# Turning softmax probabilities in a float32 mixer: a product with a scaled diagonal, or an in-place scaling and a plain transpose

## The chip, the cores and the metric

The kernel runs on one core of a Trainium2 chip. The metric is the device time of one execution in microseconds. "Line" numbers are those of the kernel before.

## What is computed

The reference sends 256 tokens of width 1024 (float32, batch 1) through a first block (retention, a linear recurrent unit, a gated feed-forward part) and then through two layers of a second block: feed-forward, hybrid mixer, feed-forward. The mixer has three branches on one input projection: gated linear attention (GLA), a causal depthwise convolution of 31 taps followed by a layer norm and silu, and sliding-window attention (8 query heads of width 64 on 2 key heads, window 128, blocks of 128, ALiBi, and one sink logit per head). For the window attention the reference computes, per head,

```python
s = jnp.einsum('bnqhgd,bnkhd->bnhgqk', qb, kk).astype(jnp.float32) * (DH ** -0.5)
s = s - slopes[:, :, None, None] * dist.astype(jnp.float32)
s = jnp.where(valid[None, :, None, None], s, -jnp.inf)
p = jax.nn.softmax(jnp.concatenate([s, sink], axis=-1), axis=-1)[..., :-1]
o = jnp.einsum('bnhgqk,bnkhd->bnqhgd', p.astype(v.dtype), vv)
```

The first query block has only its own 128 keys; the second has 256.

## The kernel before, in words

All weights are streamed from HBM in units of 1 MB (`raw`, three slots). ScalarE copies each unit to `w_hi` with a rounded type (`hi`, line 581), VectorE forms the rest `w_lo = raw - w_hi` (`lo`, line 963), and TensorE multiplies each tile three times (hi*hi, lo*hi, hi*lo). SP's queue loads unit c as soon as VectorE has split unit c - 3 (`fill`, line 388). The same two-part split is made of every activation operand (`operand_hi`, `operand_lo`: `b_hi`, `b_lo`).

Each engine has its program written out by hand, in order, with semaphores between them; nothing is reordered at run time. The mixer of layer l stands from line 1440 (VectorE), line 856 (ScalarE), line 541 (GpSimd) and from line 1958 on (TensorE); units cm to cm + 8 are its input projection, cm + 9 to cm + 12 its output projection. "Bank n" is the PSUM bank `stream[(gm + n) % 3]` in which TensorE leaves the n-th group of outputs.

The window attention is worked in two halves b = 0, 1 of four score rows each. `ss` holds, for every one of 8 slots, three blocks of 128 scores, each followed by a sink column (129 columns a block): two blocks for the second query block and one for the first. A half goes through these steps:

- VectorE adds the ALiBi table to the scores (`window_scores`, line 1472), takes the row maxima (`softmax_shift`, line 1493), and ScalarE applies the exponential in place and sums each row (`exponentials`, line 860; `ss_exp`).
- VectorE (`softmax_scale`, line 1507) takes the reciprocals of the eight row sums, waits for GpSimd's `ke_ready`, and writes eight scaled identity matrices (128x128 each) into `ek[:, 0, b]`; then it signals `p_ready`.
- TensorE (`probabilities`, line 1985) makes twelve float32 products, each with a 128x128 block of `ss` as the stationary operand and a scaled identity as the moving one. That transposes a block and divides it by its row sums at once. It signals `pt_full`; ScalarE copies the twelve tiles to `pt` (`turned_probabilities`, line 868).
- When both halves are there and all taps are done, TensorE multiplies them by the values (`window_out`, line 2098), and ScalarE and VectorE split the result for the output projection.

Among these steps, VectorE works on the taps of the convolution's first 128 channels (`conv(first, to)`, line 1444, one instruction a tap), the evacuation of bank 8 into `gr` (the GLA gate, `read_pair(8, ...)`), the head variance for GpSimd (`var8`, line 1567), the gate (line 1572), the head norm (lines 1577 and 1582) and the split of weight units (`lo`). TensorE takes the taps of the other 128 channels as products with diagonal matrices (`conv_taps`, line 1972, one tap is one float32 product of 256 columns). The order on TensorE around the change (lines 2080 to 2126) is: taps, head statistics, first half's probabilities, six taps, second half's probabilities (behind a wait for bank 8's evacuation), the roots of the heads (behind GpSimd's `rstd8_ready`), the remaining taps, `window_out` (behind both halves' copies). The output projection follows (`deep_pass`, line 1702), and between its passes the convolution's mean, variance and root.

The order on VectorE (lines 1559 to 1575):

```python
window_scores(1)
softmax_shift(1)
softmax_scale(0)
lo(cm + 10)
conv(9, 17)
dve.wait_ge(group_evac, gm + 8)
read_pair(8, gr[:, :, :], 1.0)
dve.wait_ge(stat_full, st0 + ST_GLA + 1)
V.tensor_scalar(var8[:, :], psm[:, 3, 0:8], RMS_EPS, None, ALU.add).then_inc(var8_ready, 1)
softmax_scale(1)
conv(17, 22)
```

Elsewhere the kernel turns tiles with `nc.tensor.transpose`: the residual (`turn`, line 1726, lines 1728 to 1733) and the hidden activations (line 1895), always one 128x128 tile a call.

Of the kernel before, what the change touches and what calls it, by code (L numbers as in the profile page):

```python
# [21 lines left out]
ALU = mybir.AluOpType  # L22
AX = mybir.AxisListType.X

P = 128
T = 256
TT = T // P
# [168 lines left out]
def build(nc, io, out):  # L196
    with ExitStack() as ctx:  # L197
# [23 lines left out]
        ident, means, headsel = const("ident"), const("means"), const("headsel")  # L221
# [45 lines left out]
        ek = sb("ek", [P, 2, TT, LEV, P], scope=m2)  # L267
# [6 lines left out]
        ss = sb("ss", [P, SWH, 3 * (P + 1)], scope=m2)  # L274
        mx = sb("mx", [P, 4, 16], scope=m2)
# [6 lines left out]
        def keys(slot, n):  # L282

            return ss[:, slot, n * (P + 1):n * (P + 1) + P]

        def mx_half(row, b):

            return mx[:, row, 8 * b:8 * b + 8]
# [43 lines left out]
        ez_ready, lev_ready, e_ready, qe_ready, ke_ready, zeroed, gate_ready = (sem(n) for n in (  # L332
            "ez_ready", "lev_ready", "e_ready", "qe_ready", "ke_ready", "zeroed", "gate_ready"))
# [5 lines left out]
        up_ready, diag_loaded, dve_tap, pe_taps, gla_full, gla_free, ss_ready, ss_exp, p_ready = (sem(n) for n in (  # L339
            "up_ready", "diag_loaded", "dve_tap", "pe_taps", "gla_full", "gla_free", "ss_ready", "ss_exp", "p_ready"))  # L340
# [607 lines left out]
        def _(dve):  # L948
            V = nc.vector
# [128 lines left out]
            ins = V.tensor_copy(vecs[:, :, :], stream[2][:, :].rearrange("p (g c) -> p g c", g=4))  # L1078
# [47 lines left out]
            for n in range(4):  # L1126
# [9 lines left out]
                if n == 2:  # L1136
                    dve.wait_ge(psm_full, PSM_SC + 1)
                    for h in range(HEADS):
                        ins = V.tensor_tensor(st_ret[:, 384 * h:384 * h + 384], psm[:, h, 0:384], ret_d[:, h, :], ALU.mult)
                    ins.then_inc(psm_free, 1)  # L1140

            at = [0] * KT
            for n in range(4):
# [4 lines left out]
                if n == 0:  # L1148
                    dve.wait_ge(psm_full, PSM_O + 1)
                    for h in range(HEADS):  # L1150
                        ins = V.tensor_copy(o_ret[:, 2 * h:2 * h + 2, :], pair2(psm[:, h, :]))
                    ins.then_inc(psm_free, 1)
                if n < 3:
                    tap = 2 - n
                    for k in range(KT):
                        if n == 0:
                            dve.wait_ge(lru_conv0, k + 1)
                        else:
                            dve.wait_ge(dve_chain, at[k])
                        col = V1["lconv_w"] + 8 * tap + k  # L1160
                        ins = V.scalar_tensor_tensor(out=xc[:, k, :], in0=xl[:, k, tap:tap + T],
                                                     scalar=vecs[:, 0, col:col + 1], in1=xc[:, k, :],
                                                     op0=ALU.mult, op1=ALU.add)
# [14 lines left out]
            for b in range(2):  # L1178
                ins = V.tensor_tensor(heads(o_ret, b), heads(o_ret, b), over_halves(b), ALU.subtract)
            ins.then_inc(psm_free, 1)  # L1180
            for n in range(4):
# [8 lines left out]
                if n == 2:  # L1190
                    dve.wait_ge(psm_full, PSM_VAR + 1)
                    for b in range(2):
                        ins = V.tensor_tensor(heads(o_ret, b), heads(o_ret, b), over_halves(b), ALU.mult)
                    ins.then_inc(psm_free, 1)
            for n in range(8):
# [3 lines left out]
                for f in range(2):  # L1199
                    k = 2 * (n % 4) + f  # L1200
                    if n < 4:
                        ins = V.tensor_scalar(la[:, k, :], la[:, k, :], 1.0, sp4[:, k:k + 1], ALU.add, ALU.mult)
                    else:
                        ins = V.scalar_tensor_tensor(out=i_gate[:, k, :], in0=i_gate[:, k, :], scalar=1.0,
                                                     in1=xc[:, k, :], op0=ALU.add, op1=ALU.mult)
# [6 lines left out]
            for k in range(KT):  # L1212
                ins = V.scalar_tensor_tensor(out=o_ret[:, k, :], in0=o_ret[:, k, :], scalar=half_b[:, 32 + k:33 + k],
                                             in1=g_ret[:, k, :], op0=ALU.mult, op1=ALU.mult)
# [212 lines left out]
            for l in range(LAYERS):  # L1427
# [9 lines left out]
                at = ffn(c0, 2 * l, N_L + 3 * l)  # L1437
# [6 lines left out]
                def conv(first, to):  # L1444

                    dve.wait_ge(up_ready, l + 1)
                    for tap in range(first, to):
                        acc = (yc[:, 0, :], yc_sum[:, :])[tap % 2]
                        x, w = up[:, 0, tap:tap + T], vec("conv_w", 2 * tap)
                        if tap > 1:  # L1450
                            dve.wait_ge(dve_tap, TAPS * l + tap - 1)
                        if tap == 0:
                            ins = V.tensor_scalar(acc, x, w, vec("conv_b", 0), ALU.mult, ALU.add)
                        elif tap == 1:
                            ins = V.tensor_scalar(acc, x, w, None, ALU.mult)
                        else:
                            ins = V.scalar_tensor_tensor(out=acc, in0=x, scalar=w, in1=acc, op0=ALU.mult, op1=ALU.add)
                        ins.then_inc(dve_tap, 1)
# [28 lines left out]
                def read_pair(n, dst, scale):  # L1487

                    dve.wait_ge(unit_used, USED[cm + n])
                    V.scalar_tensor_tensor(out=dst, in0=pair2(bank(n)[:, :]), scalar=scale, in1=over2(rb[:, :]),  # L1490
                                           op0=ALU.mult, op1=ALU.mult).then_inc(group_evac, 1)
# [15 lines left out]
                def softmax_scale(b):  # L1507

                    dve.wait_ge(ss_exp, 2 * l + b + 1)
                    link(V.reciprocal(mx_half(3, b), mx_half(0, b)))  # L1510
                    dve.wait_ge(ke_ready, TT * (l + 1))
                    V.tensor_tensor(ek[:, 0, b, :, :], ident.rearrange("p (o i) -> p o i", o=1).broadcast_to([P, 8, P]),
                                    mx_half(3, b).rearrange("p (n o) -> p n o", o=1).broadcast_to([P, 8, P]),
                                    ALU.mult).then_inc(p_ready, 1)

                inv_rms(ps70 + PS7_RB)
                dve.wait_ge(pool_init, 4)
# [42 lines left out]
                softmax_shift(1)  # L1560
                softmax_scale(0)
                lo(cm + 10)
                conv(9, 17)
                dve.wait_ge(group_evac, gm + 8)
                read_pair(8, gr[:, :, :], 1.0)
                dve.wait_ge(stat_full, st0 + ST_GLA + 1)
                V.tensor_scalar(var8[:, :], psm[:, 3, 0:8], RMS_EPS, None, ALU.add).then_inc(var8_ready, 1)
                softmax_scale(1)
                conv(17, 22)
                dve.wait_ge(group_evac, gm + 9)  # L1570
                dve.wait_ge(gr_th, l + 1)
                V.scalar_tensor_tensor(out=gr[:, :, :], in0=th2[:, :, :], scalar=1.0, in1=gr[:, :, :],
# [3 lines left out]
                for f in range(2):  # L1576
                    ins = V.scalar_tensor_tensor(out=og[:, f, :], in0=og[:, f, :], scalar=vec("gla_g", f),
                                                 in1=psm[:, 3, f * T:f * T + T], op0=ALU.mult, op1=ALU.mult)
# [22 lines left out]
                for f in range(2):  # L1601
                    ins = V.scalar_tensor_tensor(out=yc[:, f, :], in0=yc[:, f, :], scalar=vec("ln_g", f),
                                                 in1=cbank[:, T:2 * T], op0=ALU.mult, op1=ALU.mult)
# [33 lines left out]
        def _(pe):  # L1637
            passed = {"n": 0}

            def mm(dst, lhs, rhs, start, stop):  # L1640
                return nc.tensor.matmul(dst, lhs, rhs, start=start, stop=stop, skip_group_check=True)  # L1641
# [278 lines left out]
            for l in range(LAYERS):  # L1920
# [12 lines left out]
                def cols(tile, n):  # L1933
                    return tile[:, n * P:n * P + P]
# [50 lines left out]
                def probabilities(b, banks):  # L1985

                    pe.wait_ge(p_ready, 2 * l + b + 1)
                    for n in range(12):
                        slot, key, at = (n // 2, n % 2, n // 2) if n < 8 else (n - 8, 2, n - 4)
                        ins = mm(cols(banks[n // 4], n % 4), keys(4 * b + slot, key), ek[:, 0, b, at, :],  # L1990
                                 n % 4 == 0, n % 4 == 3)
                    ins.then_inc(pt_full, 1)

                def value(h):
# [209 lines left out]
```

## Time and profile before

| | |
|---|---|
| time, median of 3 runs | 1498.53 us (1496.96 to 1499.06) |
| the profiled execution's own time | 1498.52 us |
| span of that execution, first to last instruction | 1496.4 us |
| mean granted clock of TensorE | 0.997 of full speed |
| TensorE (PE) busy | 1467.3 us, 98% |
| VectorE (DVE) busy | 969.7 us, 65% |
| ScalarE (ACT) busy | 711.6 us, 48% |
| GpSimd (POOL) busy | 35.7 us, 2% |
| HBM | 172 GB/s over the span |

All times inside the trace count from the start of the span. PE is the row of matrix products and transposes, PEld that of the loads of their stationary operand. A start time and a duration are given for each instruction; instructions overlap in their pipelines, so what an instruction costs its engine in a dense row is the distance from its start to the next start, and not its duration. A group "x24" has the start of its first instruction and the time to the end of its last. The bracket at the end of a row is the idle time of the engine ahead of it and what ended it.

### The profile page before, as it was taken

The page shows a single profiled execution, that of the slowest core. Times are in us where ns is not written, and L with a number is a line of the kernel's source. Part 1 is how long each engine was busy: PE and PEld are TensorE (multiplying, and loading weights), DVE is VectorE, ACT ScalarE, POOL GpSimd, SP SyncE. Part 2 cuts the span into 40 slices and gives each one's busy share as a digit, 9 for nine tenths or more (in the row PEclk, how much of TensorE's full clock was granted, in tenths as well). Part 3 has the DMA queues.
Part 4 walks back from the last instruction along what each step waited for, and adds up shares of the span by engine and source line. Part 5 has one row for each costly group of instructions (what it writes and reads, how often), then busy time and mean ns, then how long its engine had stood idle before and what let it go on. Part 6 is the DMA issues. An engine that isn't in the chain of part 4 may idle for free. (4 is left out here: it accounts for less than half of the span.)

```text
span 1496.4 us, 21713 instructions
## 1 busy us (share of the span) xinstructions
PE 1467.3 (98%) x9104; PEld 1287.5 (86%) x9104; DVE 969.7 (65%) x1195; ACT 711.6 (48%) x878; POOL 35.7 (2%) x50
## 2 busy tenths in 40 slices
PE   7999999999999999999999999999999999999998
PEld 7999999899988788888987888878888889788886
DVE  5867786688864766546876665556664578666644
ACT  5433863555543544436345444354444534454442
POOL 0000000000000000001000000000000010000000
PEclk9999999999999999999999999999999999999999
DMA  7735465666655576456414755547755452365542
GB/s 249 234 120 163 147 197 192 174 179 187 180 197 169 183 225 212 154 194 148 155 57 141 219 189 183 183 143 250 225 183 185 132 136 99 113 208 179 190 156 97
DMA packets 253460, 259.15 MB, mean 173 GB/s; under 512 B 26659, under 2 KB 217524, under 8 KB 253364
## 3 DMA queue, kind: packets, MB, share of 16 engines
q1 hardware_dynamic: 252480, 255.49, 53.8%
q10 hardware_dynamic: 884, 2.28, 0.4%
q8 instruction: 72, 1.18, 0.3%
q14 instruction: 24, 0.20, 0.0%
HBM read 256.69 MB, written 1.05 MB: 172 GB/s over the span
## 5 line engine op out<-in xcount | busy, mean ns | idle before, releaser
L970 DVE TENSOR_TENSOR w_lo<-raw,w_hi 128x2048 fp32r<-128x2048 f32 x240 | 545.0, 2273 | 339.1 <-ACT w_hi L588 338.8
L588 ACT ACTIVATE w_hi<-raw 128x2048 fp32r<-128x2048 f32 x240 | 456.4, 1902 | 342.9 <-PE psm L1641 139.3
L1641 PE MATMUL stream<-a_hi,w_hi 128*128 128x256 f32 x1072 | 307.6, 287 | 2.9 <-DVE a_lo L989 1.8
L1641 PE MATMUL stream<-a_lo,w_hi 128*128 128x256 f32 x1072 | 304.6, 284 | 0.0
L1641 PE MATMUL stream<-a_hi,w_lo 128*128 128x256 f32 x1072 | 304.5, 284 | 0.0
L1641 PE MATMUL stream<-w_hi,a_hi 128*128 128x512 f32 (+1 forms) x640 | 243.6, 381 | 8.0 <-DVE w_lo L970 5.7
L1641 PE MATMUL stream<-w_hi,a_lo 128*128 128x512 f32 (+1 forms) x640 | 239.3, 374 | 0.0
L1641 PE MATMUL stream<-w_lo,a_hi 128*128 128x512 f32 (+1 forms) x640 | 238.8, 373 | 0.0
L1641 PEld LDWEIGHTS stream<-a_hi,w_hi 128*128 128x128 f32 x1072 | 206.7, 193 | 4.8 <-issue 3.2
L1641 PEld LDWEIGHTS stream<-a_lo,w_hi 128*128 128x128 f32 x1072 | 207.2, 193 | 0.0
L1641 PEld LDWEIGHTS stream<-a_hi,w_lo 128*128 128x128 f32 x1072 | 207.0, 193 | 0.0
L1641 PE MATMUL psm<-w_hi,h_hi 128*128 128x512 f32 x448 | 178.3, 398 | 0.0
L1641 PE MATMUL psm<-w_hi,h_lo 128*128 128x512 f32 x448 | 177.5, 396 | 0.0
L1641 PE MATMUL psm<-w_lo,h_hi 128*128 128x512 f32 x448 | 177.5, 396 | 0.0
L1641 PEld LDWEIGHTS stream<-w_hi,a_hi 128*128 128x128 f32 x640 | 120.5, 188 | 30.9 <-DVE w_lo L970 8.3
L1641 PEld LDWEIGHTS stream<-w_hi,a_lo 128*128 128x128 f32 x640 | 120.5, 188 | 22.0
L1641 PEld LDWEIGHTS stream<-w_lo,a_hi 128*128 128x128 f32 x640 | 120.7, 189 | 19.9
L1641 PEld LDWEIGHTS psm<-w_hi,h_lo 128*128 128x128 f32 x448 | 84.4, 188 | 20.6
L1641 PEld LDWEIGHTS psm<-w_lo,h_hi 128*128 128x128 f32 x448 | 84.4, 188 | 20.1
L1641 PEld LDWEIGHTS psm<-w_hi,h_hi 128*128 128x128 f32 x448 | 84.4, 188 | 20.1
L811 ACT ACTIVATE gu<-stream,rs 128x256 f32<-128x256 f32 x68 | 32.1, 472 | 72.2 <-PE stream L1641 72.2
L1641 PE MATMUL ps<-w_hi,a_hi 128*128 128x512 f32 x160 | 62.6, 391 | 0.0
(282 smaller groups left out, 1575.9 us busy)
## 6 DMA issues: line engine op xcount, KB each, us to landing
raw<-in_ffn_w_up SPq DMA_DIRECT2D x136, 512.0 KB, 5.0
raw<-in_ffn_w_down SPq DMA_DIRECT2D x104, 512.0 KB, 4.5
raw<-in_ffn_w_gate SPq DMA_DIRECT2D x88, 512.0 KB, 4.0
raw<-in_w_in SPq DMA_DIRECT2D x80, 512.0 KB, 4.6
raw<-in_w_out SPq DMA_DIRECT2D x24, 512.0 KB, 4.4
raw<-in_w_ret_o SPq DMA_DIRECT2D x8, 512.0 KB, 4.2
raw<-in_w_lru_o SPq DMA_DIRECT2D x8, 512.0 KB, 4.0
diag<-in_conv_diag SPq DMA_DIRECT2D x8, 512.0 KB, 5.8
```

The source lines that it names most:

```text
L588: nc.scalar.activation(w_hi[s][:, :, 0:n], raw[s][:, :, 0:n], ACT.Copy).then_inc(w_hi_ready, 1)
L811: nc.scalar.activation(th_t[:, 2 * (g % 2) + t, :], up_bank(g, t)[:, 0:UC], ACT.Tanh, scale=rs4[:, 2 + t:3 + t]).then_inc(th_ready, 1)
L970: V.tensor_tensor(w_lo[s][:, :, 0:n], raw[s][:, :, 0:n], w_hi[s][:, :, 0:n].bitcast(F32), ALU.subtract).then_inc(w_split, 1)
L1641: return nc.tensor.matmul(dst, lhs, rhs, start=start, stop=stop, skip_group_check=True)
```

## The change

The eight scaled identities are no longer made. VectorE multiplies the probabilities themselves by the reciprocals, in place in `ss`: one instruction for the four rows of 257 columns (two blocks and the sink column between them), one for the four rows of 128. The wait for `ke_ready` in this step is dropped. TensorE turns each block with `nc.tensor.transpose` and the plain identity. On VectorE the second half's scaling is moved ahead of the evacuation of bank 8, and the taps 9 to 16, which stood together ahead of the evacuation, stand behind it: 9 to 11 ahead of the head variance, 12 to 21 behind it.

```diff
--- before.py
+++ after.py
@@ -1508,10 +1508,11 @@
 
                     dve.wait_ge(ss_exp, 2 * l + b + 1)
                     link(V.reciprocal(mx_half(3, b), mx_half(0, b)))
-                    dve.wait_ge(ke_ready, TT * (l + 1))
-                    V.tensor_tensor(ek[:, 0, b, :, :], ident.rearrange("p (o i) -> p o i", o=1).broadcast_to([P, 8, P]),
-                                    mx_half(3, b).rearrange("p (n o) -> p n o", o=1).broadcast_to([P, 8, P]),
-                                    ALU.mult).then_inc(p_ready, 1)
+                    for row, first, n in ((0, 0, 2 * P + 1), (4, 2 * P + 2, P)):
+                        probs = ss[:, 4 * b:4 * b + 4, first:first + n]
+                        over = mx[:, 3, 8 * b + row:8 * b + row + 4].rearrange("p (n o) -> p n o", o=1)
+                        ins = V.tensor_tensor(probs, probs, over.broadcast_to([P, 4, n]), ALU.mult)
+                    ins.then_inc(p_ready, 1)
 
                 inv_rms(ps70 + PS7_RB)
                 dve.wait_ge(pool_init, 4)
@@ -1560,13 +1561,13 @@
                 softmax_shift(1)
                 softmax_scale(0)
                 lo(cm + 10)
-                conv(9, 17)
+                softmax_scale(1)
                 dve.wait_ge(group_evac, gm + 8)
                 read_pair(8, gr[:, :, :], 1.0)
+                conv(9, 12)
                 dve.wait_ge(stat_full, st0 + ST_GLA + 1)
                 V.tensor_scalar(var8[:, :], psm[:, 3, 0:8], RMS_EPS, None, ALU.add).then_inc(var8_ready, 1)
-                softmax_scale(1)
-                conv(17, 22)
+                conv(12, 22)
                 dve.wait_ge(group_evac, gm + 9)
                 dve.wait_ge(gr_th, l + 1)
                 V.scalar_tensor_tensor(out=gr[:, :, :], in0=th2[:, :, :], scalar=1.0, in1=gr[:, :, :],
@@ -1986,9 +1987,8 @@
 
                     pe.wait_ge(p_ready, 2 * l + b + 1)
                     for n in range(12):
-                        slot, key, at = (n // 2, n % 2, n // 2) if n < 8 else (n - 8, 2, n - 4)
-                        ins = mm(cols(banks[n // 4], n % 4), keys(4 * b + slot, key), ek[:, 0, b, at, :],
-                                 n % 4 == 0, n % 4 == 3)
+                        slot, key = (n // 2, n % 2) if n < 8 else (n - 8, 2)
+                        ins = nc.tensor.transpose(cols(banks[n // 4], n % 4), keys(4 * b + slot, key), ident)
                     ins.then_inc(pt_full, 1)
 
                 def value(h):
```

## Rows read from the trace of the kernel before

**Rows 1.** The page, part 1: busy us, share of the span, instructions.

```profile
PE 1467.3 (98%) x9104; PEld 1287.5 (86%) x9104; DVE 969.7 (65%) x1195; ACT 711.6 (48%) x878; POOL 35.7 (2%) x50
```

**Rows 2.** Busy time, 750 to 787: window; PE, PEld, DVE, ACT, POOL; PEclk, DMA, GB/s.

```profile
750.00:787.00 37.00, 37.00 (x275) 32.22 (x275) 27.00 (x49) 15.71 (x34) 2.34 (x2) 1.00 0.18 58
```

**Rows 3.** Timeline of PE in both mixers: start, duration, line, operation, out<-in, count.

```profile
757.62 2.92 PE L1641 MATMUL psm<-ek,ss 128*128 128x128 f32 x24
760.39 2.76 PE L1641 MATMUL ps<-up,diag 128*128 128x256 f32 x12
762.98 2.84 PE L1641 MATMUL stream<-ek,ss 128*128 128x128 f32 x24
765.75 1.09 PE L1641 MATMUL psm<-keep,rstd 128*64 128x128 f32 x16
...
771.29 3.11 PE L1641 MATMUL stream<-pt,vs 128*64 128x128 f32 x48
...
1258.80 2.92 PE L1641 MATMUL psm<-ek,ss 128*128 128x128 f32 x24
```

**Rows 4.** Timeline of PE: the turn of the residual's first half, projection.

```profile
796.34 0.60 PE L1732 MATMUL stream<-keep,x_t 128*128 128x128 f32 x4
796.77 0.60 PE L1732 MATMUL ps<-keep,x_t 128*128 128x128 f32 x4
797.12 0.48 PE L1641 MATMUL psm<-w_hi,b_hi 128*128 128x512 f32 x1
```

**Rows 5.** Tile x_t, PEld, 780 to 1000: duration ns min/median/max.

```profile
L1732 PEld LDWEIGHTS psm<-keep,x_t x16: 138/140/143, 806.0 to 997.3; 128*128 128x128 f32 x16
```

**Rows 6.** Timeline of DVE in the first mixer.

```profile
751.16 1.22 DVE L1512 TENSOR_TENSOR ek<-keep,mx 128x1024 f32<-128x1024 f32 x1
752.30 2.28 DVE L970 TENSOR_TENSOR w_lo<-raw,w_hi 128x2048 fp32r<-128x2048 f32 x1
754.50 0.48 DVE L1457 SCALAR_TENSOR_TENSOR yc_sum<-up,vecs,yc_sum 128x256 f32<-128x256 f32 x1
...
757.67 0.68 DVE L1490 SCALAR_TENSOR_TENSOR gr<-stream,rb 128x512 f32<-128x512 f32 x1
758.27 0.15 DVE L1567 TENSOR_SCALAR var<-psm 128x8 f32<-128x8 f32 x1
...
762.79 0.69 DVE L1572 SCALAR_TENSOR_TENSOR gr<-th,gr 128x512 f32<-128x512 f32 x1 [1.01 <-ACT th L912]
...
766.89 0.87 DVE L1577 SCALAR_TENSOR_TENSOR og<-og,vecs,psm 128x256 f32<-128x256 f32 x2 [1.44 <-PE psm L1641]
...
771.47 0.68 DVE L977 TENSOR_TENSOR b_lo<-hn,b_hi 128x512 fp32r<-128x512 f32 x1
...
772.98 0.43 DVE L1591 TENSOR_TENSOR yc<-yc,yc_sum 128x256 f32<-128x256 f32 x1
775.07 1.29 DVE L977 TENSOR_TENSOR b_lo<-stream,b_hi 128x512 fp32r<-128x512 f32 x2 [1.66 <-ACT b_hi L636]
```

**Rows 7.** Timelines of ACT and of POOL in the first mixer.

```profile
754.49 0.19 ACT L864 ACTIVATION_READ_ACCUMULATOR ss<-ss,mx 128x1 f32 x1
...
760.59 1.57 ACT L872 ACTIVATE pt<-psm 128x512 f32<-128x512 f32 x3 [4.95 <-PE psm L1641]
...
758.51 1.64 POOL L530 TENSOR_TENSOR rstd<-var,mhalf 128x8 f32<-128x8 f32 x1 [44.35 <-DVE var L1567]
```

**Rows 8.** Timeline of PE: channel mean of the convolution, first product of unit 12.

```profile
775.13 1.02 PE L1641 MATMUL stream<-yc,keep 128*128 128x256 f32 x4
...
788.05 0.47 PE L1641 MATMUL psm<-w_hi,b_hi 128*128 128x512 f32 x1 [0.28 <-DVE b_lo L977]
```

**Rows 9.** Timeline of DVE: the split of unit 13.

```profile
795.82 2.29 DVE L970 TENSOR_TENSOR w_lo<-raw,w_hi 128x2048 fp32r<-128x2048 f32 x1 [1.77 <-ACT w_hi L588]
```

**Rows 10.** Busy time of PE: window; PE; PEclk, DMA, GB/s.

```profile
15.00:20.00 5.00, 3.98 (x17) 0.67 0.99 357
796.00:798.00 2.00, 2.00 (x15) 1.00 0.00 0
```

## The prediction

> **What bounds the kernel now.** I read the page's first part first: TensorE is busy for 98% of the span and VectorE for 65% [rows 1]. Busy time alone proves nothing, since the ends of matmuls are modelled, so the next view is the busy time in the stretch of the first mixer that the change touches: over 37 us from 750 TensorE shows no idle time, at a granted clock of 1.00, while VectorE idles 10 us of it [rows 2]. The timelines of the single engines say why. TensorE goes straight from one group into the next: twelve products "psm<-ek,ss" in 24 records, six taps, twelve more products, the head roots, ten taps, the output products, the projection [rows 3]. None carries an idle bracket; in this stretch the time is the sum of what TensorE has to issue. The second layer shows the same groups, the first of them 501.18 us later and just as long [rows 3], so each term below counts twice.
>
> Two facts in these rows make the estimate. A float32 product of 128 columns takes **two records** (24 for 12), and 24 records occupy 2.77 us: 757.62 to 760.39 in the first half, 762.98 to 765.75 in the second [rows 3], or 0.231 us a product. A float32 transpose of the same size takes **one record**: a turn of the residual, two groups of four, runs from 796.34 to 797.12 [rows 4]. That is 0.78 us for eight; I add 0.10 us as my own allowance for the switch back to products, which gives 0.88 us, 0.110 each. Both forms have the data as the stationary operand and something in `keep` or `ek` as the moving one, so the change alters the mode, not the roles.
>
> **The change, part by part.**
>
> *Products become transposes (TensorE, on the path).* Removed per half: 2.77 us. Added: 12 x 0.110 = 1.32 us. Saved: 1.45 us a half, 2.90 a layer, 5.80 in all. Bounds: at worst a transpose is held to the 140 ns of its weight load [rows 5], 12 x 0.140 = 1.68, saving 1.09 a half (4.4 in all); at best the second group's pace, (797.12 - 796.77) / 4 = 0.0875, saving 1.72 a half (6.9). I take 0.110, since it covers eight transposes with the switch after them, nearest to twelve in a row.
>
> The row gives one record instead of two, a factor of 2.1. The Trainium skill (TensorE: Matmul & The Clock Gate, Terms) says that transpose mode is "4× faster for FP32". By that figure the two halves of both layers would save 4 x (2.77 - 0.69) = 8.3 us; the rows here speak for half that speed, and the sum goes by them.
>
> *Scaling the probabilities in place instead of a diagonal (VectorE, hidden, but barely).* Removed per half: one multiply of 1024 elements, 1.22 us, which holds the engine 1.14 us until the next starts (751.16 to 752.30) [rows 6]. Added: one of 1028 and one of 512. The nearest rows for 512 are the 128x512 subtraction at 771.47, 0.68 us long, and the 128x512 multiply at 757.67, which lets the next start after 0.60 [rows 6]. So a half holds VectorE 0.60 us longer, 1.20 a layer; without overlap it would be 0.68, and 0.08 more if the strided rows of the in-place form cost a start-up each. Less than 0.60 has no row in its favour, since cost goes by elements. What hides it: VectorE idles 1.01 us ahead of the gate (for ScalarE's tanh) and 1.44 us at the head norm (for TensorE's roots) [rows 6].
>
> *What the idle time becomes.* Before, VectorE reached the gate at 762.79 - 1.01 = 761.78; now at 762.98. ScalarE's tanh stands behind its copy of the turned first half, which starts at 760.59 as the products end [rows 7]; with them 1.45 us earlier, tanh ends near 761.2, so the gate waits for nothing and starts 0.19 late. The head norm was reached at 766.89 - 1.44 = 765.45; now at 765.64, and TensorE's roots, 2.90 us earlier, are done by then. It starts 1.24 us earlier than before, and all that follows on VectorE in order with it: two taps, the split of unit 11, the split of the first operand, two taps, the sum `yc`. That sum ended at 772.98 + 0.43 = 773.41 and would end at 772.17 [rows 6].
> TensorE's use of it, the channel mean, starts at 775.13 [rows 8] and would start at 775.13 - 2.90 = 772.23. Next VectorE splits the window outputs, at 775.07 after 1.66 us of idle [rows 6]; ScalarE's copy would allow that at 772.17, just when VectorE is free. So the two engines come out level, with about 0.1 us to spare. **The gain that fits is about 2.9 to 3.0 us a layer**; anything by which VectorE is dearer than 0.60 a half comes straight off it.
>
> *Moves.* The second half's scaling goes ahead of bank 8's evacuation, and five of the eight taps after that go behind the head variance. The scaling waits for the second half's exponentials: the last is read out by 754.49 + 0.19 = 754.68, while VectorE, which went on at 754.50 after the split of unit 10, now arrives at 755.10, 0.4 us after them [rows 6, 7]. Queued behind it are the evacuation of bank 8 (then ScalarE's tanh and TensorE's second half) and the head variance for GpSimd. Evacuation: 755.10 + 0.22 (reciprocal) + 1.74 = 757.06, against 757.67 before. Variance: 757.06 + 0.60 + 3 taps of 0.40 = 758.86, against 758.27 (eight taps took 754.50 to 757.67, so 0.40 each) [rows 6]. GpSimd's power takes 1.64 us [rows 7], so its result is there at 760.6; TensorE asks for it at 765.75 - 2.90 = 762.85: 2.2 us to spare. TensorE reaches the second half at 762.98 - 1.45 = 761.53 and the probabilities are ready at 757.06: no wait. The split of unit 10 slips by 0.60, and on SP's queue the load of unit 13, which waits for it; VectorE splits unit 13 at 795.82, some 40 us later [rows 9], so it costs nothing. The dropped wait on GpSimd's `ke_ready` was long fulfilled and costs nothing either.
>
> *Late next.* The conv branch chain (mean, variance, root, silu) starts from TensorE's channel mean, so it moves with TensorE; its end is the 0.28 us wait for `b_lo` at 788.05 [rows 8]. If VectorE is late by more than 0.1 us, that wait grows.
>
> **The sum.** 2 x 2.90 = 5.80 us off the profiled execution's 1498.52 us (span 1496.4 and 2.1 around it), which is the median of the runs, 1498.53. Forecast **1492.7 us**, 0.39% less. About 0.2% (3 us) is what a measurement of this kernel can tell from no change.
>
> **The rivals.**
>
> *VectorE takes part of it back.* If the in-place multiplies hold the engine x us a half longer than I charge, a layer loses 2x beyond the 0.1 us spare. At x = 0.16 (no overlap, start-ups) that is 0.2 to 0.3 a layer: 1493.3, within my range. At x = 0.75 it is 1.4 a layer and the time 1495.5, the edge of no change. Against: the in-place taps, 0.40 us for 256 elements beside 0.60 for 512 out of place, show no doubling, and the row I used for 1024 has a broadcast operand already [rows 6]. Chance of 1495.5 or more by this: 0.09.
>
> *The transposes are no cheaper.* If they ran as two records each, TensorE would save nothing, VectorE's 1.20 us would vanish in its 2.45 us of idle, and the time would be 1498.5. Every transpose in the trace has one record (four for four [rows 4]); chance 0.04.
>
> *The transposes are faster still.* At 0.0875 each TensorE would offer 3.44 us a layer; VectorE's chain passes on 3.0, giving 1492.5; with a cheaper multiply, up to 1491.6. Chance 0.07.
>
> *Slower: the granted clock falls.* Twelve transposes in a row might count as little activity, and TensorE would drop from 2.4 to 1.2 GHz at 757.6. The one fall in the trace: granted clock 0.67 over 15 to 20 us, so 3.3 us at the lower level, in the only stretch of these where TensorE also idles [rows 10]. If it stayed low from the first group to the end of the second (5.2 us of full-speed work, 10.5 at half) and 3.3 us more, 13.8 us at half speed lose 6.9 a layer: 1498.5 - 5.8 + 13.8 = 1506.5. It decides for slower from 5.8 us of low clock a layer. Against it: products and taps stand directly around the transposes, and the clock stays 1.00 across the mixer, its turn of eight included [rows 2, 10]. Chance 0.03.
> This is a rule of the Trainium skill too (TensorE: Matmul & The Clock Gate, Part 4: PE-mode transpose): full rate does not engage for transpose mode, which does not count as busy. The trace's turns do not bear it out at groups of eight.
>
> **Chances and range.** Forecast and its near surroundings 0.77, the others as given. The range runs from 1491.3 (best transposes, VectorE a little cheaper, noise of the runs of about 0.7) to 1495.5 (transposes at 0.140: 1494.1, VectorE dearer and noise on top). Faster by over 0.2%: 0.77 + 0.07 = 0.84, no change: 0.12, slower: 0.04.
>
> **What would show it.** Twelve records "<-keep,ss" instead of 24 "<-ek,ss", over about 1.3 us; VectorE pairs of 1.22 and 0.68 us; no wait ahead of the gate and the head norm on VectorE; TensorE without idle until the conv operand, there with about 0.3 us; the output products from about 768.4 instead of 771.29 [rows 3]. I am wrong in the main term if the twelve take over 1.7 us, and in the cover if a TensorE wait for `yc` or one above 0.6 us for `b_lo` appears.

## The result: 8.8 us less, and all of the surplus over the forecast lies outside the edited stretches

The changed kernel takes 1489.6 us (median of 4 runs, 1489.36 to 1490.6) against 1498.36 us (4 runs, 1496.96 to 1499.06): the ratio is 0.9947, 95% interval 0.9934 to 0.9959. The forecast was 1492.7 us with a range down to 1491.3, so the gain is half as large again as forecast, and the time is outside the range. The profiled execution took 1489.72 us, with a span of 1487.7 us.

The page of the changed kernel, part 1, beside [rows 1]: TensorE has 48 records and 6.4 us of busy time less, VectorE 4 instructions and 1.8 us more.

```profile
PE 1460.9 (98%) x9056; PEld 1280.7 (86%) x9056; DVE 971.5 (65%) x1199; ACT 711.7 (48%) x878; POOL 36.0 (2%) x50
```

TensorE's timeline in the first mixer, the rows that answer to [rows 3]. Twelve records stand where 24 stood, and the taps follow without a gap: 759.36 - 758.01 = 1.35 us for the first half, 763.35 - 761.95 = 1.40 for the second, against 2.77.

```profile
758.01 1.51 PE L1991 MATMUL psm<-keep,ss 128*128 128x128 f32 x12
759.36 2.76 PE L1642 MATMUL ps<-up,diag 128*128 128x256 f32 x12
761.95 1.47 PE L1991 MATMUL stream<-keep,ss 128*128 128x128 f32 x12
763.35 1.09 PE L1642 MATMUL psm<-keep,rstd 128*64 128x128 f32 x16
...
768.89 3.11 PE L1642 MATMUL stream<-pt,vs 128*64 128x128 f32 x48
```

The second mixer shows the same groups:

```profile
1252.84 1.51 PE L1991 MATMUL psm<-keep,ss 128*128 128x128 f32 x12
...
1263.73 3.11 PE L1642 MATMUL stream<-pt,vs 128*64 128x128 f32 x48
```

From the start of the first group to the output products the first mixer took 771.29 - 757.62 = 13.67 us before and 768.89 - 758.01 = 10.88 after: 2.79 us less. The second took (output products at 1272.46 before) 1272.46 - 1258.80 = 13.66 and now 1263.73 - 1252.84 = 10.89: 2.77 less. Together that is 5.56 us, and the forecast said 5.80. But the span fell by 8.7. Where the rest is, a ledger of landmarks along TensorE's program tells. The same group is taken in both timelines, and the difference of its start times is followed. Besides the rows shown these are the turns of the residual, before and after:

```profile
487.66 0.60 PE L1732 MATMUL stream<-keep,x_t 128*128 128x128 f32 x4
```

```profile
488.09 0.60 PE L1733 MATMUL stream<-keep,x_t 128*128 128x128 f32 x4
```

```profile
986.78 0.60 PE L1732 MATMUL stream<-keep,x_t 128*128 128x128 f32 x4
```

```profile
984.40 0.60 PE L1733 MATMUL stream<-keep,x_t 128*128 128x128 f32 x4
```

```profile
1297.50 0.60 PE L1732 MATMUL stream<-keep,x_t 128*128 128x128 f32 x4
```

```profile
1288.76 0.60 PE L1733 MATMUL stream<-keep,x_t 128*128 128x128 f32 x4
```

| landmark on TensorE | before | after | after - before |
|---|---|---|---|
| turn of the residual | 487.66 | 488.09 | +0.43 |
| first mixer, first half's probabilities | 757.62 | 758.01 | +0.39 |
| first mixer, output products | 771.29 | 768.89 | -2.40 |
| turn of the residual | 986.78 | 984.40 | -2.38 |
| **second mixer, first half's probabilities** | 1258.80 | 1252.84 | **-5.96** |
| turn of the residual | 1297.50 | 1288.76 | -8.74 |
| end of the span | 1496.4 | 1487.7 | -8.7 |

Nothing is gained or lost in the stretches between but one: from 986.78 to 1258.80, ahead of the second mixer's probabilities and in code that the change does not touch, 3.58 us disappear. With 2.79 and 2.78 in the mixers, less the 0.43 that this execution began late, that is the whole 8.7.

**What stood there.** TensorE's list of waits of the kernel before had a row that my prediction passed over:

```profile
PE psm L1641 <- issue: 1.8, 1, 1.8
```

The row says 1.8 us in all, one time, 1.8 the longest; "issue" stands for a wait that nothing else in the profile is seen to have ended. It lies in the second mixer's GLA scores. They are 60 products of 32x64 for each half of the tokens, two records each, and TensorE runs off such a burst in 1.5 us (in the changed kernel from 1221.71 to the next product at 1223.22). Before, the last 13 records of the second burst are split by such an idle bracket:

```profile
1225.26 0.34 PE L1641 MATMUL psm<-qg,kg 32*64 32x64 f32 x7
1227.41 0.34 PE L1641 MATMUL psm<-qg,kg 32*64 32x64 f32 x6 [1.80 <-issue]
```

Busy time of all engines around it, before (columns: window; PE, PEld, DVE, ACT, POOL; granted clock, DMA share, GB/s): behind the wait the granted clock is at its lower level, 1.2 GHz, for most of 1228 to 1232 (a mean of 0.57).

```profile
1224.00:1226.00 2.00, 1.53 (x114) 1.39 (x114) 1.97 (x6) 0.00 (x0) 0.00 (x0) 1.00 0.39 156
1226.00:1228.00 2.00, 0.59 (x8) 0.53 (x9) 0.13 (x1) 0.00 (x0) 0.00 (x0) 1.00 0.00 0
1228.00:1232.00 4.00, 4.00 (x23) 4.00 (x22) 3.79 (x9) 0.00 (x0) 0.00 (x0) 0.57 0.02 4
```

In the changed kernel the same burst runs through, and the clock stays at 2.4 GHz. Timeline of its last 13 records, and busy time of PE over 1210 to 1240, before and after:

```profile
1222.90 0.39 PE L1642 MATMUL psm<-qg,kg 32*64 32x64 f32 x13
```

```profile
1210.00:1240.00 30.00, 27.24 (x419) 0.94 0.33 114
```

```profile
1210.00:1240.00 30.00, 29.05 (x450) 1.00 0.46 159
```

So two costs vanished that the prediction had not counted: 1.80 us of waiting, and a stretch at half clock. A mean of 0.57 over 4 us is 3.4 us at half rate, which costs 1.7 us (0.94 over 30 us says the same within its rounding). The two make 3.5 of the 3.6 us of the ledger.

VectorE's side, which the prediction called barely covered, is read from its timeline beside [rows 6]:

```profile
751.55 1.83 DVE L1514 TENSOR_TENSOR ss<-ss,mx 128x1028 f32<-128x1028 f32 x2
753.30 2.28 DVE L970 TENSOR_TENSOR w_lo<-raw,w_hi 128x2048 fp32r<-128x2048 f32 x1
...
755.73 1.83 DVE L1514 TENSOR_TENSOR ss<-ss,mx 128x1028 f32<-128x1028 f32 x2
...
759.26 0.15 DVE L1569 TENSOR_SCALAR var<-psm 128x8 f32<-128x8 f32 x1
...
763.30 0.68 DVE L1573 SCALAR_TENSOR_TENSOR gr<-th,gr 128x512 f32<-128x512 f32 x1
...
765.88 0.86 DVE L1578 SCALAR_TENSOR_TENSOR og<-og,vecs,psm 128x256 f32<-128x256 f32 x2
...
771.89 0.43 DVE L1592 TENSOR_TENSOR yc<-yc,yc_sum 128x256 f32<-128x256 f32 x1
772.67 1.29 DVE L977 TENSOR_TENSOR b_lo<-stream,b_hi 128x512 fp32r<-128x512 f32 x2 [0.36 <-ACT b_hi L636]
```

The pair of multiplies holds the engine 753.30 - 751.55 = 1.75 us, 0.61 more than the one before. There is no idle bracket ahead of the gate (763.30) or the head norm (765.88), and the first wait is the 0.36 us for the window outputs. TensorE's channel mean and its wait for the conv operand, beside [rows 8]:

```profile
772.73 1.03 PE L1642 MATMUL stream<-yc,keep 128*128 128x256 f32 x4
...
785.64 0.47 PE L1642 MATMUL psm<-w_hi,b_hi 128*128 128x512 f32 x1 [0.27 <-DVE b_lo L977]
```

### The profile page after: what moved, and what is told of

It reads as the page before. It is cut to its first block and busy times, and to the rows that moved or that the text cites. A ratio compares the mean times of both kernels' runs of the same rounds, so it can differ in the third digit from the quotient of the medians.

```text
span 1487.7 us, 21617 instructions
## 1 busy us (share of the span) xinstructions
PE 1460.9 (98%) x9056; PEld 1280.7 (86%) x9056; DVE 971.5 (65%) x1199; ACT 711.7 (48%) x878; POOL 36.0 (2%) x50
## 3 DMA queue, kind: packets, MB, share of 16 engines
q10 hardware_dynamic: 884, 2.28, 0.4%
q8 instruction: 72, 1.18, 0.3%
```

## The experiments

Two theories for the 3.6 us. **A, the place in the stored program:** TensorE's instructions are loaded while it runs (a packet of them is under way in the middle of the burst, as the last section shows); the wait comes where the burst reaches a boundary of what has been loaded, so it depends on how many instructions stand ahead of it. The change takes out 24 records and 24 weight loads in the first mixer, which moves that boundary. **B, timing:** the second mixer starts 2.4 us earlier, or the stall is chance.

**Same count, early start (e1).** The changed kernel, and in layer 1 only:

```diff
+                def pad(n):
+
+                    for m in range(n):
+                        rows = slice(32 * (m % 3), 32 * (m % 3) + 32)
+                        mm(psm[0:64, m % 3, 0:64], ident[rows, 0:64], ident[rows, 0:64], True, True)
...
+                if l == 0:
+                    pad(12)
                 probabilities(0, [psm[:, m, :] for m in range(3)])
```

> The changed kernel plus 12 tiny float32 products (32x64 operands, results overwritten by the transposes) ahead of the first transposes in layer 1 only: TensorE's program ahead of the second mixer then has as many instructions as before the change (each such product is two loads and two records). They should cost about 0.3 us. Theory A (position of the code): the 1.8 us wait marked issue in the second mixer's GLA scores and the 3.4 us at half clock behind it come back, though the layer still starts early: 1489.6 + 0.3 + 3.5 = 1493.4 us, mean clock 0.997. Theory B (timing or chance): they stay away, 1489.9 us, mean clock 0.998.

Measured 1493.34 us (7 runs; ratio to before 0.9969, 0.9958 to 0.9981). The wait is back, at the same record of the burst, with 6 left behind it:

```profile
1227.29 0.34 PE L1642 MATMUL psm<-qg,kg 32*64 32x64 f32 x6 [1.53 <-issue]
```

```profile
15.00:20.00 5.00, 3.45 (x20) 1.00 0.98 353
280.00:295.00 15.00, 13.19 (x98) 0.89 0.59 169
1210.00:1240.00 30.00, 27.52 (x423) 0.94 0.33 116
```

Twelve tiny products, 0.6 us of TensorE's time, cost 3.7 us by the medians (3.3 by the ratios to the kernel before). It doesn't yet reject B, since the profiled execution ran late and its burst came at 1224.23, nearly where it stood before (1224.08); f1 and i1 below do. The same windows show something else: in this execution the early fall of the clock came not at 15 to 20 us but near 285. So where the clock falls early on varies from one execution to the next; this is part of the scatter of a run.

**Products with the plain identity, in both layers or one (e2, e4, e5).** The changed kernel with

```diff
-                        ins = nc.tensor.transpose(cols(banks[n // 4], n % 4), keys(4 * b + slot, key), ident)
+                        ins = mm(cols(banks[n // 4], n % 4), keys(4 * b + slot, key), ident,
+                                 n % 4 == 0, n % 4 == 3)
```

everywhere (e2), in layer 2 only (e4, so transposes in layer 1), in layer 1 only (e5).

> The changed kernel, but the twelve tiles of a half are turned by products with the plain identity instead of transposes; scaling in place on VectorE and its new order stay. Theory A: TensorE works as long as before and its program is as long, so the stall and the clock fall are there: 1498.4 us, 24 records a half, VectorE's extra 1.2 us a layer vanish in its waits. Theory B: 1498.4 as well if timing decides, 1495 if the stall is chance. If VectorE's multiplies cost more than hidden, over 1499.

> Transposes in layer 1 only, products with the plain identity in layer 2. Theory A: the program ahead of the second mixer's GLA scores is that of the changed kernel, so no stall and no clock fall there: 1489.6 + 2.8 = 1492.4 us, clock 0.998. Theory B, chance: anywhere between 1492.4 and 1496.

> Transposes in layer 2 only, products with the plain identity in layer 1. Theory A: the program ahead of the second mixer's GLA scores is as long as before, so the stall and the fall are there: 1498.4 - 2.8 = 1495.6 us, clock 0.997. Theory B, timing: the same, since that stretch also starts as late as before; chance: 1492 to 1496.

Measured: e2 1497.78 us (ratio 0.9999, 0.9989 to 1.0008), e4 1492.88 (0.9965, 0.9952 to 0.9978), e5 1494.88 (0.9980, 0.9970 to 0.9989). In e2 VectorE does all of its new work and nothing changes: the in-place scaling is free, and it brings nothing by itself. Transposes in layer 1 take off 4.9 us against e2, those in layer 2 2.9: the same edit is worth its own 2.8 in either layer, and in the first it also removes the wait of the second. (These medians put the wait and the fall at 2.0 us, less than the 3.6 of the profiled executions before and after; more on that at the end.) The windows say it in one number each, the granted clock over 1210 to 1240 (the number 0.94 or 1.00; e2, e4, e5). In e2 and e5 the wait is back at the same record, 1.53 us long; in e4 there is none:

```profile
1210.00:1240.00 30.00, 27.52 (x423) 0.94 0.32 110
```

```profile
1210.00:1240.00 30.00, 29.05 (x449) 1.00 0.46 159
```

```profile
1210.00:1240.00 30.00, 27.52 (x422) 0.94 0.34 119
```

**Nothing of the change, only shorter code (f1).** The strongest test of A, f1, takes the kernel before and shortens TensorE's program far away from everything, in its warming products at the very start:

```diff
-            spin(stream[1], 14)
+            for _ in range(3):
+                mm(stream[1][:, :], ident, x_t[:, 0, 0:512], True, True)
```

> The kernel before the change, with nothing of the change, but its 14 warming products of 128 columns at the very start replaced by 3 of 512 columns (the residual as the moving operand): about as long (3 x 0.86 against 14 x 0.23 us) but 11 products, 44 instructions of TensorE, fewer ahead of everything. Theory A (position of the code): the boundary behind the stall leaves the second mixer's burst of small products, no issue wait and no clock fall there: 1498.0 - 3.4 = 1494.6 us, clock 0.998. Theory B (the stall goes only when the layer starts earlier): 1498.0.

Measured 1494.95 us against 1497.70 (10 and 21 runs; ratio 0.9984, 0.9975 to 0.9993): 2.8 us for 44 instructions whose results nobody uses. The gain is 0.6 us smaller than expected. No issue wait is in TensorE's list, and the clock over the stretch is 1.00. This rejects B: the burst starts at the same time to 0.01 us (1224.08 before, 1224.07 here), and its last 13 records run through:

```profile
1224.08 1.33 PE L1641 MATMUL psm<-sq,ek 32*64 32x64 f32 x100 [0.39 <-DVE s_gla L1466]
```

```profile
1224.07 1.33 PE L1641 MATMUL psm<-sq,ek 32*64 32x64 f32 x100 [0.38 <-DVE s_gla L1466]
...
1225.26 0.39 PE L1641 MATMUL psm<-qg,kg 32*64 32x64 f32 x13
```

**Moving the boundary by a few instructions (f2, f3).** The kernel before with `spin(stream[1], 12)` and with `spin(stream[1], 10)`.

> The kernel before the change with 12 instead of 14 warming products at the start: 8 of TensorE's instructions fewer. If the stall stands at a fixed place of the stored program, it moves 8 instructions later in the burst: of the last 16 records 'psm<-qg,kg' 6 came behind the stall before; now 2. Length 1.4 to 1.8 us as before, time as before (1498). If it is tied to the burst itself, 6 stay.

> The kernel before the change with 10 instead of 14 warming products: 16 instructions fewer. The place of the stall then lies 2 products behind the burst, in the projection's first products. A wait is still expected there, nearly as long (the burst has used up the instructions at hand as fast as before): 1498, the issue wait in front of a 'stream<-a_hi,w_hi' or 'stream<-a_lo,w_hi' record. If it vanishes already here: 1494.8.

f2: 1498.09 us (ratio 0.9998, 0.9987 to 1.0008). The split of the burst moved as forecast, to the record: 11 and 2 instead of 7 and 6, for 4 records and 4 loads fewer ahead of it.

```profile
1225.01 0.37 PE L1641 MATMUL psm<-qg,kg 32*64 32x64 f32 x11
1227.13 0.32 PE L1641 MATMUL psm<-qg,kg 32*64 32x64 f32 x2 [1.75 <-issue]
```

f3: 1496.76 us (8 runs; ratio 0.9990, 0.9980 to 1.0001, so it is not clear of no change). The burst is through, two of the projection's products follow, and the wait stands ahead of the third, 1.28 us long; this time the clock did not fall:

```profile
1226.02 0.28 PE L1641 MATMUL stream<-a_lo,w_hi 128*128 128x256 f32 x1
1227.58 0.39 PE L1641 MATMUL stream<-a_hi,w_lo 128*128 128x256 f32 x1 [1.28 <-issue]
```

```profile
1210.00:1240.00 30.00, 27.78 (x437) 1.00 0.36 122
```

I had expected the full price there, so this was a half miss, and it is useful: it shows the wait without the fall. Where the boundary lies in the burst the wait was 1.53 to 1.80 us (1.53 in e1, e2 and e5, which ran on one chip in one batch; 1.80 and 1.75 in the others), just behind the burst 1.28, and with 44, 48 or 80 instructions taken out there was none. So the place decides whether there is a wait, and does not alone fix its length. The clock fell in the profiles with 1.5 us of it or more and not in the one with 1.28.

**Is VectorE the other limit? (g1)** The changed kernel, with the old scaled identities written as well:

```diff
+                    dve.wait_ge(ke_ready, TT * (l + 1))
+                    V.tensor_tensor(ek[:, 0, b, :, :], ident.rearrange("p (o i) -> p o i", o=1).broadcast_to([P, 8, P]),
+                                    mx_half(3, b).rearrange("p (n o) -> p n o", o=1).broadcast_to([P, 8, P]), ALU.mult)
```

> The changed kernel, but VectorE also writes the eight scaled identities as before (results unused): 1.14 us more per half, 2.28 a layer, with the wait on GpSimd that belongs to them. The trace of the changed kernel shows 0.36 to 0.41 us of spare time a layer at the window outputs and the channel mean. If VectorE is level with TensorE there (my prediction's cap), a layer loses 2.28 - 0.4 = 1.9 us: 1489.6 + 3.8 = 1493.4 us. If VectorE has ample cover: 1489.6 to 1490.2.

Measured 1493.27 us (10 runs; ratio 0.9974, 0.9965 to 0.9983), 0.1 from the estimate with VectorE level. TensorE now waits for VectorE's split of the operand, the sum `yc` and GpSimd's root, none of which it waited for in the changed kernel but 0.5 us of `b_lo`. That is 3.3 us more, of the 3.7 that were lost:

```profile
PE psm L1645 <- DVE b_lo L977: 2.9, 4, 1.2
...
PE stream L1645 <- DVE yc L1595: 0.5, 2, 0.2
PE psm L1645 <- POOL rstd L530: 0.4, 2, 0.2
```

**The move (e3).** VectorE's old order in the changed kernel:

```diff
-                softmax_scale(1)
+                conv(9, 17)
                 dve.wait_ge(group_evac, gm + 8)
                 read_pair(8, gr[:, :, :], 1.0)
-                conv(9, 12)
                 dve.wait_ge(stat_full, st0 + ST_GLA + 1)
                 V.tensor_scalar(var8[:, :], psm[:, 3, 0:8], RMS_EPS, None, ALU.add).then_inc(var8_ready, 1)
-                conv(12, 22)
+                softmax_scale(1)
+                conv(17, 22)
```

> The changed kernel with VectorE's old order: the second half's scaling behind eight taps, bank 8 and the head variance. It would end near 761.3 in the first mixer, TensorE asks for it at 761.95: level. Theory 1 (the move is only insurance): 1489.6 us, no wait of TensorE for the probabilities. Theory 2 (the move is needed): TensorE waits, up to 0.5 us a layer, 1490.6. The head variance comes 2.5 us earlier, which nobody waits for.

Measured 1489.22 us (4 runs; 0.9944, 0.9931 to 0.9958): the same. The scaling ends at 760.62, 0.6 us ahead of TensorE's second half at 761.26. The move is insurance that this kernel does not draw on.

```profile
758.88 1.83 DVE L1514 TENSOR_TENSOR ss<-ss,mx 128x1028 f32<-128x1028 f32 x2
760.62 0.48 DVE L1457 SCALAR_TENSOR_TENSOR yc_sum<-up,vecs,yc_sum 128x256 f32<-128x256 f32 x1
```

```profile
761.26 1.47 PE L1991 MATMUL stream<-keep,ss 128*128 128x128 f32 x12
```

**A version that beats both (h1, h2).** Other float32 products with the identity are transposes in disguise: those that spread a column of inverse roots over a tile. 18 of them were changed in this manner (here the one of the conv norm):

```diff
-                        ins = mm(cols(cbank, TT + t), rstd2[:, t:t + 1].broadcast_to([P, P]), ident, t == 0, t == 1)
+                        ins = nc.tensor.transpose(cols(cbank, TT + t), rstd2[:, t:t + 1].broadcast_to([P, P]), ident)
```

> The changed kernel with 18 more float32 products with the identity (the broadcast inverse roots of norms, retention heads and conv norm) issued as transposes of the broadcast column: each 0.231 - 0.112 = 0.12 us less on TensorE, 2.1 us at most; those ahead of a wait give nothing (the first two). Expected 1487.9 us (1487.4 to 1489.0). If the program's new length (up to 32 instructions shorter ahead of the second mixer's burst) puts a boundary into a burst, 1491.

> The root transposes together with VectorE's old order (the two edits that each did no harm to the changed kernel). If the orders are equal, as the single run of the old order says within its scatter, 1487.4; if the old order is worth its 0.4 us, 1487.0.

h1: 1487.43 us (5 runs; ratio 0.9932, 0.9919 to 0.9946), another 2.2 us below the changed kernel. h2: 1487.39 (4 runs; 0.9928, 0.9912 to 0.9945), so the order is worth nothing here either. The eight products of the retention heads are now eight records:

```profile
L1840 PE MATMUL psm<-keep,rstd x8: 270/272/273, 142.9 to 143.6; 128*128 128x128 f32 x8
```

**Same count, surely early (i1).** h1 with `pad(20)` in place of e1's `pad(12)`, at the same place.

> The kernel with the root transposes (1487.4 us) plus 20 tiny products in layer 1: 80 instructions, as many as the transposes of layer 1 (48) and the 16 root products ahead of the second mixer's burst (32) had taken out. The burst then starts some 2.5 to 3.5 us earlier than in the kernel before, with the same number of instructions ahead. Theory A: the wait is back at the very same record (7 and 6 of the last 16), and the fall with it: 1487.4 + 0.9 (pads) + 3.5 = 1491.8 us. Theory B (the absolute time, or the moment against the weight loads): no wait, 1488.3 us.

Measured 1491.66 us (4 runs; ratio 0.9958, 0.9939 to 0.9978). The end of the burst comes 1225.26 - 1221.58 = 3.68 us earlier than before, and it is split where it was split before, 7 and 6, by the same 1.80 us:

```profile
1221.58 0.34 PE L1642 MATMUL psm<-qg,kg 32*64 32x64 f32 x7
1223.72 0.34 PE L1642 MATMUL psm<-qg,kg 32*64 32x64 f32 x6 [1.80 <-issue]
```

## Why the prediction was wrong, point by point

*What bounds the kernel: right where I looked, and I looked at too little.* TensorE is the bound over the 37 us that I read, and all of its savings there reached the end. The step that failed is "The sum": "2 x 2.90 = 5.80 us" prices the change by the time of the instructions that it removes in the two mixers, and puts its effect on the rest of the span at nothing, without a reason. What it removes also has a number, and that number decides where in the program TensorE runs out of loaded instructions. The two missing terms are 1.80 us of issue wait and 1.7 us from the half clock in the second mixer's GLA scores, by the profiles; e1, f1 and i1 bring them or take them away without touching the work itself, and e4 and e5 do so by the layer in which the transposes stand. The sentence "The one fall in the trace" was wrong: [rows 2] and [rows 10] cover the start, the first mixer and the turn behind it, and a second fall stood at 1228 (a third, short one stands at the very end, 0.97 over 1490 to 1495). The views that would have shown it were at hand, the list of TensorE's waits and the same windows on the second layer.

*The main term: 5.56 us instead of 5.80.* Twelve transposes hold TensorE for 1.35 and 1.40 us, not 1.32. The pace of 0.110 was right: within a group a transpose starts every 0.109 us. What was missing is once per group: the first half spends 0.04 us more at its first transpose, the second 0.09 more ahead of the roots. Without the wait and the fall the kernel would have come to 1498.36 - 5.56 = 1492.8, within the range and next to the forecast. So the main term was sound, and the miss of the time is the miss of the two terms above.

*The factor of four.* The rows gave one record for two. The Trainium skill's 4x (TensorE: Matmul & The Clock Gate, Terms) would have given 8.3 us, close to the 8.8 measured, and that nearness is luck: the groups themselves shrank to a half (1.35 and 1.40 of 2.77), not a quarter.

*VectorE: right in size, the margin a little too thin.* 0.61 us more a half, as estimated, both waits gone, and a first wait of 0.36 us where I had "about 0.1 us to spare". The sum `yc` moved by 772.98 - 771.89 + 0.39 = 1.48 us, and I had 1.24. An idle bracket counts from the end of the instruction before; without a stop the next one starts about 0.08 us ahead of that end (taps of 0.48 us start every 0.40). Each stop that goes gives this back as well, and two went. That the cover is real and small g1 shows: 2.28 us of added work a layer less about 0.4 of cover gave 1493.4 on paper and 1493.27 on the chip.

*The moves.* The variance came at 759.26 - 0.39 = 758.87, forecast 758.86; nobody waited. The conv operand's wait stayed at 0.27 us.

*The rivals.* Slower by a falling clock: nothing of it; the granted clock of the changed kernel is 1.00 over 750 to 787 and over 1240 to 1275, twelve transposes in a row included. Transposes no cheaper, or cheaper still: no. VectorE taking part back: not here, but g1 is that rival made true. None of the four was what happened. (The chances given with the rivals add up to 0.13 for no change and 0.03 for slower, where the prediction's last sum has 0.12 and 0.04.)

## What to carry to other kernels

On an engine that runs without a gap, count the instructions that an edit adds or removes as well as their time: a burst of tiny products can run into the edge of the loaded program, as here, and whether it does depends on how many instructions stand ahead of it. So read every "issue" wait and every clock window of the whole span first, not of the edited stretch, and when a gain comes out larger or smaller than its terms, follow landmarks through both timelines before explaining it. And look for float32 products with an identity: as a transpose they take one record instead of two.

## What the hardware showed that was not expected

- **A wait for instructions that depends on the position in the program.** It moves by as many instructions as are taken out ahead of it (7 and 6 records became 11 and 2 for 4 records and 4 loads) and vanishes at 44 and 48. The queue list of the profile's page shows two queues of kind "instruction", and the larger has 72 packets and 1.18 MB, 16.4 KB each (the other 24 and 0.20 MB). Over TensorE's 2 x 9104 records that is about 65 bytes a record, so an estimate of 250 records a packet; one burst is 240 with its loads. That this queue is TensorE's is concluded from its size. One packet of it is under way between 1225.0 and 1226.0 before the change, none from 1226 to 1228, and the wait lasts until 1227.41. So TensorE comes to the edge while the packet is under way, and goes on more than 1.4 us after it is in. In f1 a packet comes at the same time (1225 to 1226.3), and nothing waits; by theory A TensorE comes to the edge 44 instructions later there, among the projection's products, which start only every 0.12 us. The queue over 1225 to 1226 before, and over 1225 to 1226.3 in f1:

```profile
q8 instruction: 1, 0.02, 5.7%
```

```profile
q8 instruction: 1, 0.02, 5.1%
```

The whole span, before:

```profile
q8 instruction: 72, 1.18, 0.3%
```

Why this burst stalls and the first mixer's bursts never did in these runs is argued, not shown: no run changed a burst itself.

- **A short wait can cost double.** In every profile where the issue wait was 1.5 us or longer, the granted clock fell to 1.2 GHz within some 1.5 us of its end, for about 3.4 us, at a cost of some 1.7 us. The Trainium skill (TensorE: Matmul & The Clock Gate, HAM oscillation) tells of waits between bursts of products, longer than those here, after which the clock is at half rate. The traces here agree on the level, 0.57 over 1228 to 1232, but the wait ahead of it is only 1.80 us. With 1.28 us (f3) it did not fall. One profile a kernel does not settle whether the length decides or the moment; that stays open.
- **Its price differs from run to run.** The profiles of before and after have 3.6 us for both together (those with 1.53 us of waiting 3.2); the medians give 2.0 (e4 against e5), 2.8 (f1) and about 3.2 (the change itself: 8.76 - 5.56). The kernel before shows a mean clock of 0.997 in 9 of the 21 runs beside f1 (1497.70 to 1499.17 us) and 0.998 in 12 (1496.29 to 1498.54). That the fall follows the wait in some executions and not in others would explain it; no trace of such a run was taken, so this is open too.
- **A broadcast column can be the operand of a transpose.** The roots' column, read with a stride of nothing, turns into a tile in one record of 272 ns, and h1 gained 2.2 us with it, near the 18 x 0.12 that were the estimate's most.
